# Expert weights in fewer, longer transfers: four ring slots at a time

## The reference, cut to what matters

```python
def expert_choice_moe(h, w_router, w1, w3, w2):
    aff = jax.nn.softmax(jnp.einsum('bsd,de->bse', h, w_router), axis=-1)
    cap = CAPACITY_FACTOR * S // N_EXPERTS              # 32
    gate, idx = lax.top_k(aff.swapaxes(1, 2), cap)
    xe = jax.vmap(lambda hb, ib: hb[ib])(h, idx)
    def expert(args):
        xt, w1e, w3e, w2e = args
        return (jax.nn.silu(xt @ w1e) * (xt @ w3e)) @ w2e
    ye = lax.map(expert, (xe.swapaxes(0, 1), w1, w3, w2))
    ye = ye.swapaxes(0, 1) * gate[..., None]
    ...  # added back to the rows that were chosen
```

## Time and profile before

| | |
|---|---|
| median of 3 runs | 1977.78 us (1976.65 to 1981.23) |
| the profiled execution | span 1972.5 us from its first to its last instruction; the profile gives no own total beside it. The median less the span is 5.3 us |
| busy in the span | TensorE 77%, VectorE 13%, ScalarE 11%, GpSimd 4% |
| DMA | 648.97 MB, mean 329 GB/s |
| expert weights | 384 transfers of 1408.0 KB, median 35.0 us from issue to landing |

### The profile page before, as it was taken

The page is one execution under the profiler, slowest core; times in us unless marked ns, Lnnn a source line. Parts: engine busy times, 40 slices in busy tenths (PEclk is TensorE's granted clock), DMA queues, the critical chain, the costliest instruction groups (busy, mean ns, idle before and its releaser), DMA issues.

```text
span 1972.5 us, 24615 instructions
## 1 busy us (share of the span) xinstructions
PE 1510.5 (77%) x10518; PEld 832.8 (42%) x10518; DVE 265.6 (13%) x512; ACT 225.1 (11%) x439; POOL 83.8 (4%) x88
## 2 busy tenths in 40 slices
PE   5997999999497777677677776776768767677676
PEld 3663788887354633323233232331323313223132
DVE  1115100002724300100001000010000100101001
ACT  2322122001135200000000000000000000000000
POOL 0000000000731000000000000000000000000000
PEclk8997999999797887767566676666766767767666
DMA  9458233441150489999999999999999999999998
GB/s 355 172 207 341 87 131 125 170 171 63 43 219 1 176 341 425 426 425 425 426 424 426 425 426 425 425 426 425 426 425 426 426 425 427 425 426 425 426 426 347
DMA packets 84388, 648.97 MB, mean 329 GB/s; under 512 B 7848, under 2 KB 10352, under 8 KB 35072
## 3 DMA queue, kind: packets, MB, share of 16 engines
q1 hardware_dynamic: 81296, 643.92, 78.7%
q10 hardware_dynamic: 2848, 3.54, 0.5%
q0 software_dynamic: 208, 1.00, 0.1%
HBM read 647.37 MB, written 1.06 MB: 329 GB/s over the span
## 4 chain that ended last, share of the span: by engine, by line
PE 43%; DMA 33%; SPq 16%; DVE 3%; issue 2%; POOL 2%; ACT 1%; ACTq 0%; PEldq 0%; DVEq 0%; POOLq 0%
PE ps L1048 41%; DMA ring<-in_w 31%; SPq L355 16%; POOL arena L406 2%; DMA ring<-in_w_in 1%; DVE arena L1040 1%; SPq L337 0%; PE ps L1467 0%; ACT arena L698 0%; DVE arena L855 0%; PE ps L1398 0%; PE ps L1058 0%; SPq L368 0%; ACT arena L654 0%; DMA arena<-in_w_gla_gate 0%
## 5 line engine op out<-in xcount | busy, mean ns | idle before, releaser
L1048 PE MATMUL ps<-ring,arena 128*32 128x352 f32 (+2 forms) x6914 | 762.5, 593 | 344.2 <-DMA ring<-in_w 284.6
L1048 PEld LDWEIGHTS ps<-ring,arena 128*32 128x32 f32 (+1 forms) x6914 | 243.7, 139 | 860.4 <-DMA ring<-in_w 476.9
L1048 PE MATMUL ps<-hT,ring 128*128 128x256 f32 (+1 forms) x1040 | 232.6, 385 | 11.1 <-DVE hT L857 3.9
L1048 PE MATMUL ps<-arena 128*128 (+9 forms) x972 | 196.3, 392 | 52.0 <-ACT arena L608 24.7
L1048 PEld LDWEIGHTS ps<-hT,ring 128*128 128x128 f32 (+1 forms) x1040 | 197.9, 191 | 46.5 <-issue 15.5
L1048 PEld LDWEIGHTS ps<-arena 128*128 128x128 f32 (+6 forms) x972 | 156.7, 249 | 92.9 <-issue 41.5
L1048 PE MATMUL ps<-arena,ring 128*128 128x256 f32 x768 | 168.8, 379 | 2.4 <-ACT arena L587 1.2
L1048 PEld LDWEIGHTS ps<-arena,ring 128*128 128x128 f32 x768 | 145.7, 190 | 23.3 <-issue 2.6
L698 ACT ACTIVATE arena<-ps 128x256 f32<-128x256 f32 x16 | 6.1, 384 | 809.6 <-PEq L1501 809.6
L1040 DVE TENSOR_TENSOR arena<-arena,ps 128x512 f32<-128x512 f32 x64 | 41.6, 685 | 414.4 <-PE ps L1048 414.3
L1029 DVE TENSOR_TENSOR arena<-arena,ps 128x704 f32<-128x704 f32 x16 | 14.2, 888 | 391.9 <-ACT arena L696 391.9
(11 more groups left out here) (194 smaller groups left out, 497.3 us busy)
## 6 DMA issues: line engine op xcount, KB each, us to landing
ring<-in_w SPq DMA_DIRECT2D x384, 1408.0 KB, 35.0
ring<-in_w_ff SPq DMA_DIRECT2D x8, 4096.0 KB, 13.2
ring<-in_w_ada SPq DMA_DIRECT2D x6, 4096.0 KB, 13.8
ring<-in_w_in SPq DMA_DIRECT2D x4, 4096.0 KB, 17.8
ring<-in_w_in SPq DMA_DIRECT2D x3, 2048.0 KB, 10.5
ring<-in_w_out SPq DMA_DIRECT2D x1, 4096.0 KB, 14.1
ring<-in_w_out SPq DMA_DIRECT2D x2, 2048.0 KB, 7.8
xT<-in_x_turned ACTq DMA_DIRECT2D x1, 1024.0 KB, 4.8
```

Of the source, the lines that this page charges most:

```text
L1048: return pe.matmul(o, w, x, start=first, stop=last)
```

## The change

Three things change together.

First, the features. Partition p gets rows 8 p to 8 p + 7 of w1 and w3, so that what a partition holds of a matrix is one run of 90112 bytes in memory, as it was for w2 already. The columns of `hnat` are put into the matching order by the eight ScalarE copies (now with a stride of 8 words in what they read).

Second, the transfers. An expert comes in eight pieces of (4, 4, 4, 4, 4, 2, 1, 1) slots. A piece of four slots is 128 rows of 45056 bytes. SyncE issues a piece when all slots it fills are used up, and TensorE waits once for a piece.

Third, the places in the ring. Chunk q lies in slot q % 12; units lie in block 1 + i % 3, and `ext` is the first block. The first piece covers slots 0 to 3, so it waits for `unit_used` of the unit in slot 3 too.

```diff
+PIECES = (4, 4, 4, 4, 4, 2, 1, 1)
...
-        ext = ring[:, 9 * SLOT:12 * SLOT]
+        ext = ring[:, 0:BLOCK]
...
-            o = (UNIT[name] % 3) * BLOCK
+            o = (1 + UNIT[name] % 3) * BLOCK
...
-            w1 = T["w1_2"].rearrange("e (c p) f -> p e c f", p=P)
-            w3 = T["w3_2"].rearrange("e (c p) f -> p e c f", p=P)
-            w2 = T["w2_2"].rearrange("e (p r) n -> p e (r n)", r=FR)
-
-            def chunk(e, q):
-                slot = (9 + q) % NSLOT
...
-                sp.dma_start(ring[:, slot * SLOT:(slot + 1) * SLOT], src).then_inc(chunk_in[slot], 16)
+            mats = [T["w1_2"].rearrange("e (p c) f -> p e (c f)", p=P), T["w3_2"].rearrange("e (p c) f -> p e (c f)", p=P),
+                    T["w2_2"].rearrange("e (p r) n -> p e (r n)", r=FR)]
+
+            def piece(e, i):
+                q, n = PIECE_AT[i]
+                at, mat = q % NSLOT, q // C
+                sp.dma_start(ring[:, at * SLOT:(at + n) * SLOT],
+                             mats[mat][:, e, (q - C * mat) * SLOT:(q - C * mat + n) * SLOT]).then_inc(piece_in[i], 16)
+
+            def block_free(slot):
+                return UNIT["wout"] + 1 if slot < 3 else len(UNITS) - 3 + slot // 3
+
+            for i, (q, n) in enumerate(PIECE_AT):
+                if q < NSLOT:
+                    sp.wait_ge(s["unit_used"], block_free(q + n - 1))
                 else:
-                    src = w2[:, e, (q - 2 * C) * SLOT:(q - 2 * C + 1) * SLOT]
+                    sp.wait_ge(s["w_used"], q + n - NSLOT)
+                piece(0, i)
             with sp.Fori(0, NE - 1) as e:
+                for i, (q, n) in enumerate(PIECE_AT):
+                    sp.wait_ge(s["w_used"], NCHUNK * e + q + n + NCHUNK - NSLOT)
+                    piece(e + 1, i)
...
-                    src = bk(f"hn{i}").rearrange("p (c st d) -> p c st d", c=2, st=ST)[:, :, st, :]
-                    A(hnat[:, st, 2 * i * P:(2 * i + 2) * P].rearrange("p (c d) -> p c d", c=2), src,
-                      ACT.Copy).then_inc(s["hnat_set"], 1)
+                    src = bk(f"hn{i}").rearrange("p (c st a b) -> p st b c a", c=2, st=ST, b=C)[:, st, :, :, :]
+                    dst = hnat[:, st, :].rearrange("p (b i c a) -> p i b c a", b=C, i=4, c=2)[:, i, :, :, :]
+                    A(dst, src, ACT.Copy).then_inc(s["hnat_set"], 1)
...
-                        pe.wait_ge(chunk_in[slot], 32 * e + 16 * (q // NSLOT + 1))
+                        if q in PIECE_OF:
+                            pe.wait_ge(piece_in[PIECE_OF[q]], 16 * (e + 1))
```

More of the change, by code:

```diff
@@ L67 @@
 NVEC = sum(n for _, n in VEC.values())
+PIECE_AT = [(sum(PIECES[:i]), n) for i, n in enumerate(PIECES)]
+PIECE_OF = {q: i for i, (q, n) in enumerate(PIECE_AT)}
+assert sum(PIECES) == NCHUNK and all(q % C + n <= C and q % NSLOT + n <= NSLOT for q, n in PIECE_AT)
 def bank_plan():
@@ L254, in build @@
         unit_in2 = sem("unit_in_gate_columns")
-        chunk_in = [sem(f"chunk_in{q}") for q in range(NSLOT)]
+        piece_in = [sem(f"piece_in{i}") for i in range(len(PIECES))]
         s = {name: sem(name) for name in """
@@ L338, in _ @@
                 if name == "win_a":
[L339 removed]
+                    o = (1 + i % 3) * BLOCK + C * 512
                     sp.dma_start(ring[:, o:o + C * RANK].rearrange("p (c n) -> p c n", c=C),
                                  rows(T["w_in"], 1536, RANK)).then_inc(unit_in2, 16)
[L343 to L345 removed]
@@ L347, in chunk @@
-            def chunk(e, q):
-                slot = (9 + q) % NSLOT
[L349 to L352, removed]
-                else:
-                    src = w2[:, e, (q - 2 * C) * SLOT:(q - 2 * C + 1) * SLOT]
-                sp.dma_start(ring[:, slot * SLOT:(slot + 1) * SLOT], src).then_inc(chunk_in[slot], 16)
[L358 to L363, removed]
@@ L364, in _ @@
-            with sp.Fori(0, NE - 1) as e:
[L365 to L375, removed]
+            mats = [T["w1_2"].rearrange("e (p c) f -> p e (c f)", p=P), T["w3_2"].rearrange("e (p c) f -> p e (c f)", p=P),
+                    T["w2_2"].rearrange("e (p r) n -> p e (r n)", r=FR)]
@@ L1136, in _ @@
             w = unit_ap("win_a", C, 512)
-            o = (UNIT["win_a"] % 3) * BLOCK + C * 512
+            o = (1 + UNIT["win_a"] % 3) * BLOCK + C * 512
             wg = ring[:, o:o + C * RANK].rearrange("p (c n) -> p c n", c=C)
@@ L1473, in _ @@
                         q = mat * C + c
-                        slot = (9 + q) % NSLOT
-                        pe.wait_ge(chunk_in[slot], 32 * e + 16 * (q // NSLOT + 1))
+                        slot = q % NSLOT
+                        if q in PIECE_OF:
+                            pe.wait_ge(piece_in[PIECE_OF[q]], 16 * (e + 1))
                         w = ring[:, slot * SLOT:(slot + 1) * SLOT]
@@ L1486, in _ @@
                 pe.wait_ge(s["pgT_set"], e + 1)
-                w2v = ring[:, 1 * SLOT:9 * SLOT].rearrange("p (r n) -> p r n", r=FR)
+                w2v = ring[:, 4 * SLOT:12 * SLOT].rearrange("p (r n) -> p r n", r=FR)
                 got = 0
```

## The result

The changed kernel takes 1962.39 us (median of 4 runs, 1959.59 to 1963.62); the kernel before took 1978.93 us in the same comparison. The ratio is 0.9919, with an interval of 0.9906 to 0.9933: about 16 us faster, where 8.3 were forecast.

The account below looks back on a forecast made before the run. The DMA stream of expert weights was taken to bound the kernel. Fewer packets gave -11.8 us and the later restart +3.5, so -8.3: span 1964.2, median 1969.5 us, ratio 0.996; range 1961 to 1984.

Parts of the forecast that it names:

- so I take 5.3 ns: Weight stream: each packet costs 5.3 ns beside its bytes; 144 fewer save 0.76 us an expert, 11.8 us in all.
- The upper bound of 8.2 ns: Weight stream: highest cost of a packet, from the time packets occupied, counting overlap twice; up to 18.3 us saved.
- The first pieces: Stream start: the first three pieces go out after 646.22 and are loaded by 690; nothing lost.
- The late restart: Idle stream in expert 0: its restart waits for four chunks used instead of one; +3.5 us.
- Waits in the loop: Expert loop: coarser releases stay covered by two queued pieces, about 16 us to spare; cost nothing.
- The `hnat` copies: ScalarE before the experts: eight copies at twice the price add 2.6 us, within 11.98 us idle; zero.
- The tail: After the last landing: unchanged at 9.7 us, taken as 0; +2.6 us at most if the clock halves.
- That the rate does not rise: Loop stream: 425 GB/s is a limit or rows are cut; 1980 to 1981.3 us; 0.25 together with too small a gain.
- Rival 2: Loop stream: whole occupied time per packet goes, 8.2 ns; -14.8 us, so 1963.0; chance 0.17 with what lies between.
- Long rows that stream worse: Loop stream: reading long rows from far-apart places costs 1.4 us an expert; +25 us, 2003; 0.13 shared with other cases.
- A starved queue: Loop stream: runs dry if a release comes over 16 us late; called small, 0.13 shared with other cases.
- The carried-over offset: Whole kernel: median of runs 5.3 us above the profiled span, carried over to turn 1964.2 us into 1969.5.

Follow-up runs that it names:

- old-rows run: Changed kernel's transfers with the old feature order and `hnat` copies: w1 and w3 in 11264-byte rows, w2 keeping long rows; 1974.76 us, ratio 0.9992.
- quarter slots: Changed kernel's layout with one-slot transfers, each cut in four: 96 an expert, rows of 2816 bytes; 2059.71 us, ratio 1.0411.
- one slot: Changed kernel with transfers of one slot again, 24 an expert, rows of 11264 bytes, new feature layout and ring places kept; 1977.85 us, ratio 0.9996.
- the end not cut: Changed kernel with pieces of (4, 4, 4, 4, 4, 4), without the final 2 + 1 + 1; 1967.70 us, ratio 0.9940.
- half and quarter slots: Changed kernel's layout with one-slot transfers cut in two (5632-byte rows; 2004.62 us, ratio 1.0133) or in four (2816-byte rows; 2059.71 us, ratio 1.0411).

## Why the prediction was right in kind and short by half

**The bound and the mechanism** held. The stream sets the time of the loop, the number of packets sets what the stream takes beyond its bytes, 216 become 72, and 372 chunks lie behind the restart. The page's DMA share and the 1152 packets show it; the old-rows run shows that it is the rows and not the number of transfers.

**The term that was mis-sized** is "so I take 5.3 ns". It measures 8.4 ns: 144 x 8.4 = 1.21 us an expert and 18.8 us in all, where the sum had 11.8. With the restart at +3.7 and the tail at -0.4 that makes -15.5, and the counted difference is 14.8 + 0.4 = 15.2; the medians say 16.5. That the forecast reached half of the gain is owed to the right count of packets, not to their price.

The 5.3 came from two windows of 6 and 3 us in the dense blocks, set against the full stream. There short rows read faster than the line above: it gives 412 GB/s for 4096 bytes and 392 for 2048, those rows read 418 and 402. The full stream at 5632 and 2816 bytes lies on the line, so length alone is not the reason. But the windows were short for the purpose. With 604 packets in place of 612, half a packet less for each engine, the prediction's algebra gives 8.3 ns in place of 4.8, and windows of 6 us that begin at 10.5 and 12 us count 615 and 610. Whether rows in the dense blocks are really cheaper, or the windows were too short to tell, is open.

The upper bound of 8.2 ns, from occupied time, comes out near the measured value by chance. Within the stream the same reading gives too much: 103.6% of 86.74 us with the quarter slots against 101.0% of 81.33 with one slot is 11.9 ns a packet, 8.4 of period and 3.5 of overlap. So the prediction was right that occupied time counts overlap twice; the fast dense rows happened to hide it.

**The Trainium skill's 3 cycles a packet** (3.5 ns, an estimate; "DMA: Bandwidth & Descriptors", section "Why small descriptors are slow (HBM only)") are less than half of what these runs show. The Trainium skill's 425 GB/s for a core streaming alone ("HBM Reference", "Specifications (TRN2)") is what 11264-byte rows give and no ceiling: rows of 45056 bytes give 432 here and 433 with the end not cut.

**The first pieces.** The prediction took the earlier trace rows to begin with the fourth chunk. The 31 issues from 646.22 on begin with the seventh: three chunks went out from 558.7 and three from 577.6. So the first piece did not wait until 646.22 but went out at 582.9, and all twelve slots were full at 683.6. The slip changes no term of the sum.

**The late restart** was foreseen at +3.5 and measures 3.7 in the trace, and 3.3 to 3.6 when taken out. **Waits in the loop** cost nothing: the DMA share stays at a 9, and the first streamed piece lands 16.9 us after its issue, where 15.9 were foreseen. **The `hnat` copies** still take 0.66 us a pair. **The tail** was not slowed by the clock; it came out 0.4 us shorter, at a higher clock.

**The rivals.** That the rate does not rise: refuted. Rival 2, the whole occupied time: its 1963.0 us is the measured time within 1 us, and it had 0.17 of the chance with all that lies between. But its mechanism is not what happened, since by occupied time the stream would have gained 11.9 ns a packet; the number is right by luck. Long rows that stream worse: refuted by the 432 GB/s and by the one-slot run in the new layout. A starved queue: no slice shows one.

**The carried-over offset.** "The median is 5.3 us above the profiled span" was taken as a constant of the measurement. In the runs of the study the time of an execution is 1.8 us above its own span. The other 3.5 us fit that execution's early start of the experts, 695.77 where other profiles have up to 702.48: the one-slot kernel, with the same period, starts them 3.9 us later and has a span 3.6 us longer. The executions that were only timed have no such row, so this is an inference. The offset did not hurt the ratio, but it makes two single spans comparable only after that start is taken out.

## What to carry to other kernels

Where a stream of weights keeps the DMA engines full, count packets: the period is the bytes plus a fixed price for each packet, here 8.4 ns (or 9.4 ns for each row of weights alone). Lay out memory so that a partition's rows join into one run; by the old-rows kernel, large transfers do not help the matrices whose rows stay short. A coarser transfer has two prices outside the steady state, the restart of an idle stream and the work behind the last landing, and both are avoided by splitting the transfer there and only there. Take a per-packet price from long stretches of the same kind as the one it is meant for, and ask first how far one packet more or less in the window would move it.

## What the runs showed of the hardware that was not expected

TensorE's granted clock rose though nothing was done for it. In one expert it reads 0.67 before (1082.2 to 1152 us, TensorE busy for 48.43 us) and 0.77 after (41.86 us busy for the same 434 records). With single chunks TensorE worked 2.58 us and waited 0.8 us again and again at the half level of 1.2 GHz; with pieces it works 6.6 to 7.6 us and then idles for nearly 6. The experiments show that the size of the transfers does it and not the length of rows: over 1000 to 1400 us the clock reads 0.67 with one slot, 0.73 with two, and 0.76 both in the changed kernel and with the old rows in large transfers. It is off the path here. The window of the kernel before, to set beside the one from 1085.00 above:

```profile
1082.20:1152.00 69.80, 48.43 (x434) 15.47 (x434) 3.56 (x3) 2.94 (x5) 0.76 (x2) 0.67 1.01 426
```

SyncE's issue of a transfer took a median of 2718 ns before and 333 ns after, for as many rows each. Before, some ten transfers of 128 rows stood in the queue; now there are two or three. The line-355 view of before and the line-342 view of after:

```profile
L355 SPq DMA_DIRECT2D ring<-in_w x384: 327/2718/6817, 558.7 to 1926.0; - x192
```

```profile
L342 SPq DMA_DIRECT2D ring<-in_w x128: 327/333/343, 582.9 to 1918.3; - x128
```

No run was made for this, but the traces of the others say something. With two slots a transfer (192 transfers, a median of 35.1 us to landing, so about five in the queue) the median issue is 333 ns. The half and quarter slots, with eleven or twelve transfers in the queue, have 1343 and 693 ns. In the old-rows kernel a large transfer of w1 or w3 is 512 rows, so that about as many rows stand in the queue as before, and its issue takes 368 to 399 ns. So it is hardly the rows in the queue. The long issues come where ten or more transfers stand in it, and their median is 0.77 to 0.80 of the time in which one transfer of their kind streams (3.39, 1.73 and 0.90 us), as if SyncE waited for one of them to leave. That is a reading, not a test.
